# Head sums in two fp32r halves one pass later, and a read moved behind the inverse's copies, in a hybrid decoder layer

## The chip, the cores and the metric

The kernel runs on one core of a Trainium2 chip. The metric is the device time of one execution in microseconds (us). Engines are named as the profile names them: PE is TensorE, PEld its weight loads, DVE is VectorE, ACT is ScalarE, POOL is GpSimd, SP issues the DMAs.

## What is computed

One layer of a hybrid decoder, on 512 prompt tokens and 8 x 8 sample tokens (576 in all), width 1024, 8 heads. Cut to what matters here:

```
h = rmsnorm(x); proj = h @ w_in            # q|k|v | beta | decay | z | GLU input (2x) | gates a, b
q, k, v = silu(causal_conv4(proj)); q, k = l2norm(q) * 128**-0.5, l2norm(k)
per head, chunks of tokens:  lhs = I + strict(beta * k k^T * decay)
    u = solve(lhs, beta * v) - ...;  S = gl * S + ko^T u;  o = qd S + (q k^T * decay) u
o = o * rsqrt(mean(o*o) + eps) * delta_norm_g * silu(z)
c = causal_conv31(glu); o_b = silu(layernorm(c))
x = x + rmsnorm((sigmoid(a)*o + sigmoid(b)*o_b) @ w_out)
y = x + rmsnorm(relu(rmsnorm(x) @ w_up)**2 @ w_down)
```

## The kernel before

Channels lie on the 128 partitions, tokens along the free dimension, in two halves of 288 columns. Each projection is a **job**: 48 matmuls of 128x288, for each half 8 blocks of channels times three products (high weight by high input, low by high, high by low, all fp32r). Even halves of all jobs share one PSUM bank and odd halves another (`dense_ps`), so the first matmul of a job's half waits until the same half of the job before has been read (`act_read`), and half 0 also for its weights (`w_high` by ACT, `w_low` by POOL).

The head recurrence runs in **passes** `phase(n)`, n = 1 to 8, one for each head, beside the projection of the next head: passes 1 to 7 carry 7 jobs (q, k, v, then CA and CB, the two GLU halves, then Z and GA), pass 8 carries 10. A pass has 32 **slots** s, 2 us each or so. In slot s each engine runs what stands for it there, in program order: PE first issues `MIDDLE_AT[s]` dense matmuls, then the head's step. Passes 2 to 7 on PE, ACT, POOL and 4 to 7 on DVE are a loop. The steps that the text needs:

- Slot 0: PE sums k's squares over channels with a matrix of ones (`ones_pair`, two fp32r halves, L775 and L776), ACT makes the factor by Ln and Exp (L1490, L1492), DVE scales k (L1905). Slot 2: transposes of k and v on PE (L868 and on), DVE makes `gk`.
- Slots 8 to 21: the inverse of the 64x64 blocks, level by level. On even slots PE multiplies `t_r` by a level's part of the matrix (L920, at level 7 in slot 18 L918), ACT copies the product to `x_r`; on odd slots PE multiplies by `x_r` (L940, at slot 19 L938), DVE subtracts from `t_r` and transposes. In slot 18 ACT copies `x_r` (L1511) and then `u_r` (L1514), for which PE waits at L938.
- Slots 22 to 30: the chunks of the recurrence. The output o stands in PSUM; ACT copies it and squares it, DVE adds to the squares (slot 30, `o_sq`). In slot 30 PE makes the sample states' update (L1015), which DVE adds to `ss` (`sample_state`). In slot 31 PE sums o's squares with `ones_sum`, one fp32 product for each half (L768), ACT makes the factor (L1568, L1570) and q's squares (L1389), DVE scales o in two operations.
- ACT reads each job's halves in the slot after they are done: half 0 in `evac_first`, half 1 in `evac`. Half 0 of job 4 (CB, by a sigmoid) is read in slot 18, ahead of `x_r` and `u_r`. Its reader's table is loaded ahead of it.
- DVE works off the 31 taps of the Conformer convolution of the prompt (L1908, 128x512) in portions set by the tables `early` (the last taps of the head before) and `late` (the first taps of this one); passes 1, 2, 3 and 8 have tables of their own. The samples' taps are multiplied on POOL in two halves (slots 10 and 14; 2 and 4 in pass 8) and summed by a DVE reduction over 31 (L2036; slots 14 and 16, or 3 and 6).

In slot 19 of the loop PE has eleven dense matmuls. The last of them is the first of job 5, and behind it stands L938:

```order
L734 REGISTER_ALU
L743 ISA [waits w_low,w_high]
L749 MATMUL ps<-in_hi,w_hi 128x288 [waits act_read]
L931 REGISTER_ALU [waits x_ready]
L938 MATMUL ps<-x_r,u_r 64x64 [waits uc_ready]
L938 MATMUL ps<-x_r,u_r 64x64 x3
```

It is the row with `act_read`: for it half 0 of job 4 must have been read. The changed kernel has the same order here.

## Time and profile before

| | us |
|---|---|
| three runs | 1057.59, 1057.67, 1058.25 |
| median | 1057.67 |
| the profiled execution | 1057.45 |
| its span, first to last instruction | 1055.7 |
| PE busy in the span | 1038.3 |
| DVE, POOL, ACT busy | 745.4, 634.6, 592.1 |

So 1.75 us of the profiled execution lie outside the span. Passes 1 to 8 end at 116.7, 186.7, 252.5, 317.9, 383.3, 448.7, 514.0 and 598.1 us, if the start of L1015 is taken as the end; behind them come the output projection and the feed-forward part. The granted TensorE clock is 1.000 of full speed throughout. Matmuls overlap in the records, so distances between starts tell what one costs: dense matmuls start 0.13 us apart.

### The profile page before, as it was taken

The page shows a single profiled execution, that of the slowest core. Times are in us where ns is not written, and L with a number is a line of the kernel's source. Part 1 is how long each engine was busy: PE and PEld are TensorE (multiplying, and loading weights), DVE is VectorE, ACT ScalarE, POOL GpSimd, SP SyncE. Part 2 cuts the span into 40 slices and gives each one's busy share as a digit, 9 for nine tenths or more (in the row PEclk, how much of TensorE's full clock was granted, in tenths as well). Part 3 has the DMA queues.
Part 4 walks back from the last instruction along what each step waited for, and adds up shares of the span by engine and source line. Part 5 has one row for each costly group of instructions (what it writes and reads, how often), then busy time and mean ns, then how long its engine had stood idle before and what let it go on. Part 6 is the DMA issues. An engine that isn't in the chain of part 4 may idle for free.

```text
span 1055.7 us, 21847 instructions
## 1 busy us (share of the span) xinstructions
PE 1038.3 (98%) x7971; PEld 1012.8 (96%) x7971; DVE 745.4 (71%) x1254; ACT 592.1 (56%) x1105; POOL 634.6 (60%) x546
## 2 busy tenths in 40 slices
PE   8999999999999999999999999999999999999997
PEld 6999989999999999999999999999999999999997
DVE  7989898898888988889867757594544444444335
ACT  7855556575565755656646865765444443343632
POOL 1894686684876948768583443646555555555631
PEclk9999999999999999999999999999999999999999
DMA  6312212222122221322222162122222223222402
GB/s 239 105 68 81 95 42 92 84 80 95 40 91 84 79 95 40 93 81 90 88 77 61 43 250 80 41 70 97 98 96 81 81 83 114 82 79 79 116 7 89
DMA packets 32651, 92.08 MB, mean 87 GB/s; under 512 B 4688, under 2 KB 12240, under 8 KB 32592
## 3 DMA queue, kind: packets, MB, share of 16 engines
q1 hardware_dynamic: 32592, 91.29, 26.2%
q8 instruction: 37, 0.61, 0.2%
q14 instruction: 22, 0.18, 0.1%
HBM read 82.76 MB, written 8.52 MB: 86 GB/s over the span
## 4 chain that ended last, share of the span: by engine, by line
PE 80%; DVE 7%; POOL 4%; issue 3%; ACT 2%; DVEq 0%; ACTq 0%; POOLq 0%
PE ps L749 26%; PE ps L1162 15%; PE ps L1110 13%; PE ps L758 7%; PE ps L1194 5%; PE ps L714 3%; DVE ps L1908 3%; DVE t_r L1905 1%; PE ps L1006 1%; POOL in_lo L2601 1%; DVE work L2139 1%; PE ps L768 1%; POOL work L2601 1%; POOL w_lo L2601 1%; POOL o_a L2601 1%
## 5 line engine op out<-in xcount | busy, mean ns | idle before, releaser
L2601 POOL TENSOR_TENSOR w_lo<-raw,w_hi 128x1024 fp32r<-128x1024 f32 x100 | 241.2, 2414 | 157.0 <-ACT w_hi L1734 50.2
L749 PE MATMUL ps<-in_hi,w_hi 128*128 128x288 f32 x944 | 286.1, 303 | 1.1 <-ACT work L1408 0.6
L749 PE MATMUL ps<-in_lo,w_hi 128*128 128x288 f32 x944 | 282.3, 300 | 0.7 <-POOL in_lo L2601 0.7
L749 PE MATMUL ps<-in_hi,w_lo 128*128 128x288 f32 x944 | 282.7, 300 | 0.0
L1908 DVE SCALAR_TENSOR_TENSOR ps<-work,ct,ps 128x512 f32<-128x512 f32 x240 | 180.5, 752 | 7.1 <-DVE work L2068 1.6
L749 PEld LDWEIGHTS ps<-in_hi,w_hi 128*128 128x128 f32 x944 | 177.7, 188 | 2.7 <-issue 1.2
L749 PEld LDWEIGHTS ps<-in_lo,w_hi 128*128 128x128 f32 x944 | 177.3, 188 | 1.0 <-POOL in_lo L2601 0.9
L749 PEld LDWEIGHTS ps<-in_hi,w_lo 128*128 128x128 f32 x944 | 177.6, 188 | 0.5
L1905 DVE TENSOR_TENSOR o_a<-o_a,ps 128x576 f32<-128x576 f32 (+1 forms) x63 | 42.8, 681 | 107.3 <-PE ps L1162 73.1
L2601 POOL TENSOR_TENSOR w_lo<-t_pair,w_hi 128x1024 fp32r<-128x1024 f32 x18 | 43.6, 2422 | 42.5 <-ACT w_hi L1763 29.7
L1291 ACT CAST w_hi<-raw 128x1024 fp32r<-128x1024 f32 x63 | 65.6, 1043 | 0.2
L1162 PE MATMUL ps<-f_hi,w_lo 128*128 128x288 f32 x288 | 61.8, 296 | 0.0
L1162 PE MATMUL ps<-f_hi,w_hi 128*128 128x288 f32 x288 | 61.8, 296 | 0.0
L1162 PE MATMUL ps<-f_lo,w_hi 128*128 128x288 f32 x288 | 61.8, 295 | 0.0
L1908 DVE SCALAR_TENSOR_TENSOR ps<-work,qt,ps 128x512 f32<-128x512 f32 x72 | 54.0, 751 | 1.8
L2601 POOL TENSOR_TENSOR work<-work 128x576 f32<-128x576 f32 (+3 forms) x37 | 47.1, 1283 | 11.1 <-PE ps L996 7.9
L1162 PEld LDWEIGHTS ps<-f_hi,w_lo 128*128 128x128 f32 x288 | 46.3, 189 | 0.0
L1162 PEld LDWEIGHTS ps<-f_lo,w_hi 128*128 128x128 f32 x288 | 46.3, 189 | 0.0
L1162 PEld LDWEIGHTS ps<-f_hi,w_hi 128*128 128x128 f32 x288 | 46.2, 189 | 0.0
L1905 DVE TENSOR_TENSOR t_pair<-raw 128x1024 f32<-128x1024 f32 x24 | 45.1, 1880 | 0.0
L1734 ACT CAST w_hi<-raw 128x1024 fp32r<-128x1024 f32 x18 | 18.9, 1052 | 46.4 <-PE ps L1162 37.3
L1905 DVE TENSOR_TENSOR q_sq<-ps,q_sq 128x288 f32<-128x288 f32 x24 | 11.0, 458 | 47.4 <-PE ps L1110 46.9
(396 smaller groups left out, 2862.3 us busy)
## 6 DMA issues: line engine op xcount, KB each, us to landing
raw<-w_all_in SPq DMA_DIRECT2D x135, 512.0 KB, 3.7
work<-s_in_in SPq DMA_DIRECT2D x8, 512.0 KB, 3.4
s_sample_out<-work SPq DMA_DIRECT2D x8, 512.0 KB, 2.6
xt<-x_t_in SPq DMA_DIRECT2D x4, 576.0 KB, 6.4
xt<-x_t_in SPq DMA_DIRECT2D x2, 1152.0 KB, 7.1
y_out<-o_a SPq DMA_DIRECT2D x14, 144.0 KB, 1.9
halo<-halos_in SPq DMA_DIRECT2D x9, 156.0 KB, 3.5
conf_rows_out<-c_rows SPq DMA_DIRECT2D x8, 135.0 KB, 3.4
```

The costliest lines, as they stand in the source:

```text
L714: r = mm(ps[:, 2 * w + h, 0:HALF], a[:, k], b[:, k, h * HALF:(h + 1) * HALF], start=k == 0 and p3 == 0, stop=k == KB - 1 and p3 == 2)
L749: t = mm(dense_ps(n, j, h), a[:, w, k], b[:, k, h * HALF:(h + 1) * HALF], start=r == 0, stop=r == PASS_MM // 2 - 1)
L758: r = mm(dst, a[:, k], half_of(b[:, k], h), start=k == 0 and p3 == 0, stop=k == KB - 1 and p3 == 2)
L768: r = mm(dst[:, h], ones_r[:].bitcast(F32), src[:, h * HALF:(h + 1) * HALF], start=start, stop=stop)
L1110: r = mm(dst, a[:, k], b[:, k], start=start and k == 0 and p3 == 0, stop=k == 3 and p3 == 2, skip_group_check=True)
L1162: r = mm(job_ps(i % 2)[:, h], a[:, k], half_of(b[:, 4 * odd + k], h), start=k == 0 and p3 == 0, stop=k == 3 and p3 == 2)
L1194: r = mm(half_ps(i % 4), a[:, k], half_of(b[:, k], h), start=i < 2 * H - 1 and k == 0 and p3 == 0, stop=k == ks_end and p3 == 2, skip_grou ...
L1291: nc.scalar.copy(w_hi[:, w_buf(n, j)], raw[:, raw_slot(n, j)]).then_inc(w_high, 1)
L1734: nc.scalar.copy(ring(s)[0], raw[:, slot]).then_inc(w_high, 1)
L1905: return ve.tensor_tensor(out, a, b, op)
L1908: return ve.scalar_tensor_tensor(out=out, in0=a, scalar=s_, in1=b, op0=op0, op1=op1)
L2601: return gp.tensor_tensor(out, a, b, op)
```

## The change

The line numbers of the profile are of the kernel before.

```
+        osq_hi = ... [P, TOK] F32R at starts["vt"];  osq_lo = ... at starts["qn"]
@@ PE, slot 0 @@
+                            pe.wait_ge(o_sq, 2 * n - 2)
+                            pe.wait_ge(o_read, 5 * n - 5)
+                            ones_pair(g2(2), osq_hi, osq_lo).then_inc(o_sums, 1)
@@ PE, slot 2 @@
+                        if not n_is(n, 1):
+                            pe.wait_ge(o_log, n)
...
-                    if s == (30 if last(n) else 31):
+                    if last(n) and s == 30:
@@ ACT @@
-                for s in range(33):
+                def read_first(s):
                     pos, j = evac_first(n, s)
...
+                for s in range(33):
+                    if last(n) or s != 18:
+                        read_first(s)
...
+                    if s == 18 and not last(n):
+                        read_first(s)
...
-                    if s == (11 if last(n) else 24 if n_is(n, 1) else 19):
+                    if s == (11 if last(n) else 25 if n_is(n, 1) else 19):
...
                         A(g2(0), g2(0), ACT.Exp, scale=-0.5).then_inc(k_scale, 1)
+                        if not n_is(n, 1):
+                            act.wait_ge(o_sums, n - 1)
+                            A(two(v["at"]), g2(2), ACT.Ln, ...).then_inc(o_log, 1)
+                            act.wait_ge(o_log, n)
+                            A(v["at"], v["at"], ACT.Exp, scale=-0.5).then_inc(o_scale, 1)
+                            square_q(n - 1)
...
                     if s == 31 and not last(n):
+                        act.wait_ge(o_sq, 2 * n - 1)
+                        A(osq_hi[:], v["gk"][:, 0:TOK], ACT.Copy).then_inc(o_read, 1)
                         log_exp()
-                        act.wait_ge(o_sums, n)
-                        A(two(v["at"]), g2(2), ACT.Ln, ...).then_inc(o_log, 1)
-                        act.wait_ge(o_log, n + 1)
-                        A(v["at"], v["at"], ACT.Exp, scale=-0.5).then_inc(o_scale, 1)
-                        square_q(n)
@@ DVE @@
-                ve.tensor_reduce(..., conf_products(), ...)
+                ve.tensor_reduce(..., conf_products()[:, :, :, CF_TAPS // 2:CF_TAPS], ...)
+            def squares_low(n):
+                dve.wait_ge(o_read, 5 * n)
+                tt(osq_lo[:], v["gk"][:, 0:TOK], osq_hi[:].bitcast(F32), ALU.subtract).then_inc(o_sq, 1)
-                if s == 31 and not last(n):
...
+            def scale_head(n):
+                dve.wait_ge(o_scale, n)
...
+                tt(v["db"], o, v["at"], ALU.mult).then_inc(o_scaled, 1)
...
+                stt(o, v["db"], pcol("delta_g", 0), v["zs"], ALU.mult, ALU.mult).then_inc(head_out, 1)
...
                 if s == 30 and not last(n):
                     sample_state(n)
+                    squares_low(n)
...
+                    if not n_is(n, 1) and s == 1:
+                        scale_head(n - 1)
-            early = {1: 4, 2: 1, 3: 2, 8: 1, 14: 1, 16: 1}
+            early = {0: 1, 1: 1, 2: 2, 3: 2, 8: 2, 14: 1, 16: 2, 18: 1}
-            early_2 = {1: 4, 2: 2, 3: 2, 8: 2, 9: 1, 10: 1, 12: 1, 14: 1, 16: 1, 18: 2}
+            early_2 = {0: 1, 1: 1, 2: 2, 3: 2, 8: 2, 9: 1, 12: 1, 14: 2, 16: 2, 18: 4}
@@ POOL, behind the samples' products @@
+                        pool.wait_ge(conv31_p, 4 * n - 3 + 2 * half)
+                        m_ = CF_TAPS // 2
+                        tt(conf_products()[:, :, :, m_:2 * m_], conf_products()[:, :, :, m_:2 * m_],
+                           conf_products()[:, :, :, 0:m_], ALU.add).then_inc(conv31_p, 1)
```

The sum of o's squares moves from slot 31, as fp32, to slot 0 of the next pass, as two fp32r halves: ACT writes the high half in slot 31, DVE the low half behind `sample_state`. K's factor and scaling now come ahead of o's. The late tables lose a tap or two (`late` 21 to 19, `late_1` 14 to 13, `late_2` 19 to 17) and the early ones gain as many. The samples' products are added pairwise on POOL, 15 of 31, and DVE reduces 16. In pass 8, where o's squares stay fp32, DVE runs the head's step ahead of the layer norm's in each slot, and ACT squares behind the copies of the inverse.

On ACT, slot 18 of the loop, before and after. The conversion of job 6's weights leads, the read of job 4's half 0 is the sigmoid L1397, L1404 in the new numbering:

```order
L1291 CAST w_hi<-raw 128x1024 [waits job_done,raw_landed2]
L1438 REGISTER_ALU
L1397 ACT_TABLE_LOAD [waits zs_ready]
L1397 ACTIVATE work<-ps 128x288 [waits job_done]
L1511 ACTIVATE x_r<-ps 64x4x64 [waits x_ps]
L1514 ACTIVATE u_r<-work 64x4x64 [waits ui_ready]
L1514 ACTIVATE u_r<-work 64x4x64
```

```order
L1298 CAST w_hi<-raw 128x1024 [waits job_done,raw_landed2]
L1523 ACTIVATE x_r<-ps 64x4x64 [waits x_ps]
L1526 ACTIVATE u_r<-work 64x4x64 [waits ui_ready]
L1526 ACTIVATE u_r<-work 64x4x64
L1445 REGISTER_ALU
L1404 ACT_TABLE_LOAD [waits zs_ready]
L1404 ACTIVATE work<-ps 128x288 [waits job_done]
```

The table load and the read now stand behind the three copies to `x_r` and `u_r`.

On PE, at the end of the loop's body, before and after, with the dense matmuls of slot 0 left out behind the first:

```order
L1015 MATMUL ps<-work 128x512 [waits s_ready,um_ready]
L1015 MATMUL ps<-work 128x512
L768 MATMUL ps<-work,ones_r 128x288 [waits o_read,o_sq]
L768 MATMUL ps<-work,ones_r 128x288
L1041 REGISTER_ALU
L1041 COMPARE_AND_BRANCH
L749 MATMUL ps<-in_hi,w_hi 128x288 [waits act_read,w_low,w_high]
```

```order
L1022 MATMUL ps<-work 128x512 [waits s_ready,um_ready]
L1022 MATMUL ps<-work 128x512
L1048 REGISTER_ALU
L1048 COMPARE_AND_BRANCH
L751 MATMUL ps<-in_hi,w_hi 128x288 [waits act_read,w_low,w_high]
```

L768 is gone from between the state's update (L1015, now L1022) and the first dense matmul. In slot 0, behind the dense matmuls, there is now, from the last of k's four on:

```order
L778 MATMUL ps<-ksq_lo,ones_r 128x288
L777 MATMUL ps<-osq_hi,ones_r 128x288 [waits o_read,o_sq]
L778 MATMUL ps<-osq_lo,ones_r 128x288
L777 MATMUL ps<-osq_hi,ones_r 128x288
L778 MATMUL ps<-osq_lo,ones_r 128x288
```

The four matmuls on `osq` are new here; k's four stood here alone before, as L775 and L776.

On DVE, from `sample_state` in slot 30 on (128x1024), at the end of the loop's body, before and after:

```order
L1905 TENSOR_TENSOR work<-work,ps 128x1024 [waits ss_decayed,ss_ps]
L2028 REGISTER_ALU
L1908 SCALAR_TENSOR_TENSOR ps<-work,ct,ps 128x512 [waits conv31]
L2028 REGISTER_ALU
L1908 SCALAR_TENSOR_TENSOR ps<-work,ct,ps 128x512 [waits conv31]
L1905 ISA [waits o_scale]
L1905 TENSOR_TENSOR work<-o_a,work 128x576
L1908 SCALAR_TENSOR_TENSOR o_a<-work,par 128x576 [waits zs_ready,o_scaled]
```

```order
L1921 TENSOR_TENSOR work<-work,ps 128x1024 [waits ss_decayed,ss_ps]
L1921 TENSOR_TENSOR osq_lo<-work,osq_hi 128x576 [waits o_read]
L2044 REGISTER_ALU
L1924 SCALAR_TENSOR_TENSOR ps<-work,ct,ps 128x512 [waits conv31]
L2044 REGISTER_ALU
L1924 SCALAR_TENSOR_TENSOR ps<-work,ct,ps 128x512 [waits conv31]
L2337 REGISTER_ALU
L2337 COMPARE_AND_BRANCH
L1921 TENSOR_TENSOR work<-work,ps 128x576 [waits k_scale]
```

The new `osq_lo` comes directly behind `sample_state`. Before, o's two operations (`o_scale`, `o_scaled`) stood here; now the last row, k's scaling of the next pass, is ahead of them, and they stand behind two more taps.

## Rows read from the trace of the kernel before

**Rows 1.** The page, busy time, share of the span and instructions of PE.

```profile
PE 1038.3 (98%) x7971; PEld 1012.8 (96%) x7971; DVE 745.4 (71%) x1254; ACT 592.1 (56%) x1105; POOL 634.6 (60%) x546
```

**Rows 2.** Stretches, passes 1, 2, 5, 8: length, busy PE, PEld, DVE, ACT, POOL, clock.

```profile
48.00:116.67 68.67, 65.65 (x519) 62.98 (x517) 61.05 (x113) 42.88 (x89) 53.11 (x63) 1.00 0.24 80
116.67:186.66 69.99, 67.20 (x525) 63.51 (x524) 61.58 (x110) 38.78 (x82) 47.68 (x52) 1.00 0.22 75
...
317.90:383.30 65.40, 65.12 (x525) 63.44 (x524) 57.76 (x104) 38.79 (x82) 46.12 (x52) 1.00 0.25 78
...
514.04:598.06 84.02, 82.80 (x652) 80.93 (x651) 59.96 (x103) 57.63 (x101) 51.38 (x38) 1.00 0.24 77
```

**Rows 3.** Waits, all engines: who waited for whom, us in total, times, longest.

```profile
PE ps L938 <- ACT u_r L1514: 1.6, 6, 0.3
PE ps L980 <- DVE work L1908: 0.7, 1, 0.7
```

**Rows 4.** Timeline at the end of pass 5: start, us, engine, line, operation.

```profile
384.35 1.24 PE L768 MATMUL ps<-work,ones_r 128*128 128x288 f32 x4
384.47 1.22 DVE L1905 TENSOR_TENSOR work<-work,ps 128x1024 f32<-128x1024 f32 x1 [0.93 <-PE ps L1015]
385.21 0.51 PE L749 MATMUL ps<-in_hi,w_hi 128*128 128x288 f32 x1
385.56 0.30 PE L749 MATMUL ps<-in_hi,w_lo 128*128 128x288 f32 x1
387.01 0.30 PE L775 MATMUL ps<-ksq_hi,ones_r 128*128 128x288 f32 x1
...
387.54 0.29 PE L749 MATMUL ps<-in_hi,w_hi 128*128 128x288 f32 x1
```

**Rows 5.** Timeline, pass 6: DVE's step of slot 9, PE's of slot 10.

```profile
408.77 0.21 DVE L1905 TENSOR_TENSOR work<-work,ps 64x64 f32<-64x64 f32 x1
...
409.08 0.43 PE L920 MATMUL ps<-t_r,x_last 128*64 128x128 f32 x4
```

**Rows 6.** Timeline, pass 6, slots 18 and 19, of ACT and PE.

```profile
423.40 1.28 ACT L1397 ACT_TABLE_LOAD   x1
424.33 0.37 PE L918 MATMUL ps<-t_r,x_last 128*64 128x64 f32 x4
424.69 0.41 ACT L1397 ACTIVATE work<-ps 128x288 f32<-128x288 f32 x1
425.13 0.38 ACT L1511 ACTIVATE x_r<-ps 64x256 fp32r<-64x256 f32 x1
425.53 0.85 ACT L1514 ACTIVATE u_r<-work 64x256 fp32r<-64x256 f32 x2
...
425.95 0.29 PE L749 MATMUL ps<-in_hi,w_hi 128*128 128x288 f32 x1
426.52 0.39 PE L938 MATMUL ps<-x_r,u_r 128*64 128x64 f32 x4 [0.28 <-ACT u_r L1514]
```

**Rows 7.** Timeline, pass 8, the same step, where ACT has no read ahead of it.

```profile
564.33 0.39 PE L918 MATMUL ps<-t_r,x_last 128*64 128x64 f32 x4 [1.22 <-issue]
564.76 0.38 ACT L1511 ACTIVATE x_r<-ps 64x256 fp32r<-64x256 f32 x1 [1.24 <-PE ps L918]
...
566.03 0.41 ACT L1399 ACTIVATE gate<-ps 128x288 f32<-128x288 f32 x1
```

**Rows 8.** Timeline of PE, pass 2, slots 5 and 12.

```profile
132.83 0.40 PE L749 MATMUL ps<-in_hi,w_hi 128*128 128x288 f32 x1 [0.57 <-ACT work L1408]
...
149.07 0.43 PE L920 MATMUL ps<-t_r,x_last 128*64 128x128 f32 x4 [0.65 <-issue]
```

**Rows 9.** Groups by form: count, busy us, mean ns of one, idle before.

```profile
L1908 DVE SCALAR_TENSOR_TENSOR ps<-work,ct,ps 128x512 f32<-128x512 f32 x240 | 180.5, 752 | 7.1 <-DVE work L2068 1.6
L2036 DVE TENSOR_REDUCE work<-work 128x32 f32<-128x992 f32 x16 | 19.0, 1185 | 1.0 <-POOL work L2601 0.6
L2601 POOL TENSOR_TENSOR work<-work 128x576 f32<-128x576 f32 x16 | 22.7, 1417 | 3.1 <-ACT work L1397 3.1
```

More of the change, by code:

```diff
@@ L189, in build @@
         ksq = v["extk"][:, 4:4 + TOK]
+        osq_hi = nc.alloc_sbuf_tensor_at("osq_hi", [P, TOK], F32R, offset=work_at + 4 * (5 * SEQ + starts["vt"]))
+        osq_lo = nc.alloc_sbuf_tensor_at("osq_lo", [P, TOK], F32R, offset=work_at + 4 * (5 * SEQ + starts["qn"]))
         q_sq = sb("q_sq", TOK)
@@ L1475, in phase @@
                         A(job_ps(1), job_ps(1), ACT.Copy, scale=1.0 / D).then_inc(mu_ready, 1)
-                    if last(n) and 15 <= s < 19:
-                        for k in (2 * s - 30, 2 * s - 29):
-                            act.wait_ge(xc_ready, k + 1)
-                            A(xc_squares(k), conf[:, k], ACT.Square).then_inc(xc_sq, 1)
                     if last(n) and s == 21:
@@ L1492, in phase @@
                         A(g2(0), g2(0), ACT.Exp, scale=-0.5).then_inc(k_scale, 1)
+                        if not n_is(n, 1):
+                            act.wait_ge(o_sums, n - 1)
+                            A(two(v["at"]), g2(2), ACT.Ln, scale=1.0 / P, bias=con("epsq")).then_inc(o_log, 1)
+                            act.wait_ge(o_log, n)
+                            A(v["at"], v["at"], ACT.Exp, scale=-0.5).then_inc(o_scale, 1)
+                            square_q(n - 1)
                     if s == 2 and not n_is(n, 1):
@@ L1524, in phase @@
                             conv_silu(n, 0)
+                    if s == 18 and not last(n):
+                        read_first(s)
+                    if last(n) and 15 <= s < 19:
+                        for k in (2 * s - 30, 2 * s - 29):
+                            act.wait_ge(xc_ready, k + 1)
+                            A(xc_squares(k), conf[:, k], ACT.Square).then_inc(xc_sq, 1)
                     if s == 22:
@@ L1562, in phase @@
                         A(dst, g(3), ACT.Copy).then_inc(o_read, 1)
-                        act.wait_ge(o_read, 4 * n - 1)
+                        act.wait_ge(o_read, 5 * n - 2)
                         A(g(3), g(3), ACT.Square).then_inc(o_read, 1)
                     if s == 31 and not last(n):
+                        act.wait_ge(o_sq, 2 * n - 1)
+                        A(osq_hi[:], v["gk"][:, 0:TOK], ACT.Copy).then_inc(o_read, 1)
                         log_exp()
-                        act.wait_ge(o_sums, n)
-                        A(two(v["at"]), g2(2), ACT.Ln, scale=1.0 / P, bias=con("epsq")).then_inc(o_log, 1)
-                        act.wait_ge(o_log, n + 1)
-                        A(v["at"], v["at"], ACT.Exp, scale=-0.5).then_inc(o_scale, 1)
-                        square_q(n)
             act.preload_act_table_set("sigmoid_and_others")
@@ L2034, in conf_samples @@
                 at = SEQ + half * n_ * LS
-                dve.wait_ge(conv31_p, 2 * h + half + 1)
-                ve.tensor_reduce(v["c31"][:, at:at + n_ * LS].rearrange("p (s a) -> p s a", s=n_), conf_products(),
+                dve.wait_ge(conv31_p, 4 * h + 2 * half + 2)
+                ve.tensor_reduce(v["c31"][:, at:at + n_ * LS].rearrange("p (s a) -> p s a", s=n_),
+                                 conf_products()[:, :, :, CF_TAPS // 2:CF_TAPS],
                                  mybir.AxisListType.X, ALU.add).then_inc(conv31_s, 1)
@@ L2237, in phase @@
                 for s in range(32):
+                    if last(n) and 22 <= s < 26:
+                        for k in (2 * s - 44, 2 * s - 43):
+                            if k == 0:
+                                dve.wait_ge(ln_scale, 2)
+                            tt(two(conf[:, k]), two(conf[:, k]), job_ps(1), ALU.mult).then_inc(ln_scaled, 1)
+                    if n_is(n, 1) and s == 0:
+                        dve.wait_ge(in_ready, KB)
+                    head(n, s)
                     if last(n) and 14 <= s < 18:
@@ L2246, in phase @@
                         tt(xc_squares(k), xc_squares(k), xc_squares(k + 1), ALU.add).then_inc(xc_pair, 1)
-                    if last(n) and 22 <= s < 26:
-                        for k in (2 * s - 44, 2 * s - 43):
-                            if k == 0:
-                                dve.wait_ge(ln_scale, 2)
-                            tt(two(conf[:, k]), two(conf[:, k]), job_ps(1), ALU.mult).then_inc(ln_scaled, 1)
-                    if n_is(n, 1) and s == 0:
-                        dve.wait_ge(in_ready, KB)
-                    head(n, s)
                     if not n_is(n, 1) and s == 0:
```

31 lines of the change are left out of this document (14 added, 17 removed).

## The prediction

> **What bounds the kernel now.** The page comes first: PE is busy in 1038.3 of the 1055.7 us of its span [rows 1]. So an edit counts only by what it does to PE's own work and to the places where PE stands still. The stretches by pass say where those are. A steady pass (5) takes 65.4 us with 0.28 us of PE idle; pass 1 has 3.0 us idle, pass 2 takes 4.6 us more than pass 5 and has 2.8 us idle, and pass 8 has 1.2 us [rows 2]. These are idle times of the pipelined records, and the distances between starts show somewhat more. The waits name the steady one: L938 waits for ACT's u_r, 0.3 us six times [rows 3]. In the timeline L938 starts 0.57 us behind the dense matmul ahead of it, where a head step otherwise follows at the dense step of 0.13 us, so the true stop is 0.44 us [rows 6]. The other engines have room.
>
> **o's sum (7 passes).** L768 starts at 384.35 and the second dense matmul behind it at 385.56, 1.21 us. Without it a dense step of 0.13 and the change from fp32 to fp32r, for which I take 0.15, are left, so it costs 0.93. The four fp32r matmuls that replace it cost what k's four cost, 387.54 - 387.01 = 0.53 [rows 4]. Gain 0.40 a pass, **-2.8 us**; bounds 0.3 to 0.55. Does PE wait for them? sample_state ends at 385.69; osq_lo behind it, priced as a tap of 0.75 [rows 9], ends at 386.45. PE would come to o's sum at 387.01 - 0.93 + 0.53 = 386.6 [rows 4]. It just fits; 0.2 us later it would not. ACT's new copy and the factor of o stand behind k's factor, where PE's next use of the bank is slot 2, some 3 us on: nothing.
>
> **What DVE gives back of it.** In slot 9 DVE's last step on the samples ends at 408.98 and PE's L920 starts at 409.08: PE runs at DVE's pace there [rows 5]. DVE comes to it with nearly as much work as before: osq_lo and a second tap in slot 8 are new, three taps ahead of slot 2 are gone and one is added in slot 2. I take DVE 0.2 us earlier and PE 0.4, so 0.2 is lost in each of the five steady passes: **+1.0 us**; bounds 0 and the whole 2.8.
>
> **The read behind the copies (7 passes).** This is the large term. Before, ACT loads the sigmoid's table at 423.40, while it waits anyway, and reads job 4's half 0 from 424.69 to 425.10, then copies x_r and u_r until 426.38 [rows 6]. Now the copies come first. When would they? Pass 8 shows this step without a read ahead: L1511 starts 0.43 us behind L918's start, and the next read on ACT 1.70 us behind it, with no table to load [rows 7]. So in passes 1 to 7 the load starts at L918 + 1.70, lasts until + 2.98, and the read of 0.41 ends at + 3.40. The copies alone would be ready for L938 by + 1.66, where PE is at + 1.75: the old stop of 0.44 would go. But the last dense matmul of slot 19, ahead of L938, is job 5's first and waits for this read. PE reaches it at 425.95 - 424.33 = 1.62 behind L918; with the 0.14 us from ACT's end to PE's start (426.38 to 426.52) it can start only at + 3.54 [rows 6]. PE stands 1.92 us, and L938 follows at + 3.67 instead of + 2.19. Net 1.48 us a pass, seven times: **+10.4 us**. Nothing hides it, since PE is the bound and its queue is in order. In pass 2 four taps of 0.75 in slot 18, two more than before, keep DVE busy to about the same point, so PE's next head steps come no earlier there either. Bounds: 1.2 if ACT's steps run tighter together, 1.6 if PE restarts more slowly.
>
> Of the table the trace shows that the activation behind it starts 1.29 us after it began (423.40 to 424.69), the load's own 1.28 and no more [rows 6]. The Trainium skill ("ScalarE: Activation LUTs", What ACT_TABLE_LOAD costs) has about 1283 ns for the load and a drain of about 1380 ns with every switch. By the page the stop would be 1.38 us longer each time, and the sum 9.7 us higher.
>
> **Pass 1.** L980 waits 0.7 us for DVE [rows 3]; the new stop of 1.9 us ahead of it gives DVE the time to catch up, and a tap leaves slot 10. I take **-1.0 us** of the 3.0 idle [rows 2]; bounds 0 and -2.
>
> **Pass 2, ahead of slot 18.** It loses its time because DVE is late. At 132.83 a dense matmul starts 0.57 us late since ACT, held by DVE's difference, reads its bank late; at 149.07 L920 comes 0.65 late, behind a tap too many in slot 10 [rows 8]. The change brings k's scaling forward by some 2 us (o's factor and scaling are no longer ahead of it), takes the tap out of slot 10, and halves the reductions of 1.19 us [rows 9]. Of the 4.6 us over pass 5 [rows 2] about 0.9 lie behind slot 18; of the other 3.7 I take **-3.0 us**; bounds -1.5 and -3.7.
>
> **Pass 8.** L918 waits 1.22 us [rows 7] for DVE's t_r, which stood behind two layer-norm subtractions and a sum of pairs. They now come behind it, but the variance chain behind is as long, and L953 stands at its end: **-0.8 us**; bounds 0 and -1.4.
>
> **POOL's additions.** 480 elements a partition, between a third and all of the 1.42 us of 576 [rows 9], twice a pass. Behind the second stands the low half of job 5's weights, which DVE's shorter reduction lets start earlier. Nothing on PE: 0, bounds 0 and +2.
>
> Sum: -2.8 + 1.0 + 10.4 - 1.0 - 3.0 - 0.8 = **+3.8 us**. The profiled execution took 1057.45 us, its span 1055.7 and 1.75 around it; with the sum 1061.25. It is 0.2 below the median of 1057.67, which would give 1061.5. I say 1061.3.
>
> **Rivals.** *The read is in time.* If ACT's read were over before PE needs the bank, 1.62 us behind L918, the stop would not come and the old one of 0.44 would go in six passes, -2.6, while pass 2's taps keep +1.4. Then -2.8 + 1.0 - 1.2 - 1.0 - 3.0 - 0.8 = -7.8, **1049.7**, faster. For it: the change is made at just the place where PE waits for u_r. Against: the order of ACT and of PE around it, and 1.70 + 1.28 + 0.41 against 1.62. It decides at a read that ends 1.5 us behind L918. Chance 0.12.
>
> *The stops heal each other.* The 1.9 us stop in passes 1 and 2 lets DVE catch up wholly, the sum's gain is kept, pass 8 gains all: -2.8 + 10.4 - 2.2 - 4.6 - 1.4 = -0.6, **1056.9**, within 0.2%. For it: all three passes wait for DVE. Against: the stop is late in the pass, and what is lost ahead of it is lost. Chance 0.10.
>
> *DVE and POOL are later still.* The sum's gain is given back whole at slot 10 (+1.8), pass 2 gains half: 3.8 + 1.8 + 1.5 = +7.1, or with POOL's bound +9: **1066**. Chance 0.10.
>
> *A drain with the table.* A switch of tables also waits for the pipeline to empty, behind copies that have only just ended: 3.8 + 7 x 1.38 = +13.5, **1071**. Against: the 1.29 us of the row, though there ACT had nothing fresh in its pipe. Chance 0.03. It is the page's rule on the drain, and by that rule the trace does not agree.
>
> **How the numbers follow.** Forecast 0.65, centre 1061.3, from its bounds 1058 to 1065. The range 1056.5 to 1066.5 holds the forecast, the healed case and most of the slow one. It leaves out the read in time, the drain and half of the slow case, about 0.2. A measurement of this kernel tells some 0.2% (2.1 us) from no change. Faster: 0.12 and a little of the healed case, 0.14. Same: the rest of that and the forecast's lower edge, 0.13. Slower 0.73.
>
> **What would show it.** In the changed profile: the dense matmul ahead of the step on x_r and u_r in slot 19 waits for ACT's sigmoid read, 1.6 to 2 us by start distances, seven times; a steady pass takes 65.4 - 0.2 + 1.5 = 66.7 us, pass 2 about 68.3, pass 1 about 69; the four matmuls on osq follow k's at 0.13 us each with no gap; pass 8's wait at level 7 is gone. It is wrong if steady passes come out below 65.4: then ACT's read was not what PE waited for.

## The result, and the profile after

The changed kernel took **1084.57 us** in the median of its runs (1084.21 to 1086.61), beside 1057.84 (1057.59 to 1058.25) for the kernel before on the same chip: ratio 1.0256, 95% interval 1.0238 to 1.0274. The prediction said slower, but 1061.3 us, and its range ended at 1066.5.

The profiled execution of the changed kernel took 1084.21 us, its span is 1082.4, 26.7 more than before. Of its page the row of PE, which answers [rows 1]:

```profile
PE 1045.0 (97%) x7971; PEld 1019.0 (94%) x7971; DVE 754.5 (70%) x1261; ACT 594.9 (55%) x1112; POOL 659.2 (61%) x562
```

PE's busy time grew by 6.7 us although it has the same number of matmuls and cheaper ones, and 20 us are new idle time. Busy time that grows with the same work points to a slower clock. The stretches by pass, which answer [rows 2] (length, busy PE, PEld, DVE, ACT, POOL, then the granted clock), show where:

```profile
48.00:121.48 73.48, 67.15 (x522) 64.94 (x520) 60.87 (x114) 43.18 (x89) 57.17 (x65) 0.98 0.23 75
121.48:191.46 69.98, 66.62 (x524) 63.36 (x523) 61.42 (x110) 39.29 (x83) 49.41 (x54) 1.00 0.23 75
191.46:259.12 67.66, 65.54 (x525) 63.38 (x524) 59.80 (x107) 39.20 (x83) 49.38 (x54) 1.00 0.23 76
259.12:326.09 66.97, 65.16 (x524) 63.33 (x523) 58.36 (x105) 39.20 (x83) 49.40 (x54) 1.00 0.23 77
326.09:394.71 68.62, 66.78 (x524) 64.92 (x523) 58.47 (x105) 39.19 (x83) 49.38 (x54) 0.98 0.23 75
...
463.31:530.38 67.07, 65.25 (x524) 63.38 (x524) 58.40 (x105) 39.20 (x83) 49.38 (x54) 1.00 0.24 76
530.38:624.39 94.01, 85.15 (x652) 83.00 (x651) 66.24 (x105) 57.85 (x102) 54.10 (x40) 0.95 0.22 69
```

Passes 1 to 8 are 4.8, 0.0, 1.8, 1.6, 3.2, 3.2, 1.7 and 10.0 us longer than before, and what is behind them 0.4. Two kinds of steady pass stand side by side, 67 us and 68.6, and the second kind has a clock below 1.00. Pass 8 alone has more than a third of the loss.

**The steady stop.** Pass 5, slots 18 and 19, of ACT and PE, the rows that answer [rows 6]:

```profile
368.13 0.84 ACT L1526 ACTIVATE u_r<-work 64x256 fp32r<-64x256 f32 x2
368.99 1.28 ACT L1404 ACT_TABLE_LOAD   x1
370.29 0.41 ACT L1404 ACTIVATE work<-ps 128x288 f32<-128x288 f32 x1
368.82 0.29 PE L751 MATMUL ps<-in_lo,w_hi 128*128 128x288 f32 x1
370.75 0.40 PE L751 MATMUL ps<-in_hi,w_hi 128*128 128x288 f32 x1 [1.64 <-ACT work L1404]
370.99 0.37 PE L945 MATMUL ps<-x_r,u_r 128*64 128x64 f32 x4
```

The dense matmul behind 368.82 starts 1.93 us later instead of 0.13, since the read of job 4 now stands behind the copies and the table load: 1.80 us of stop, and its predecessor's records end 1.64 before it. It comes in each of passes 1 to 7. The activation starts 1.30 us behind the start of its table load, and the load 0.02 us behind the end of fresh copies: the load's own 1.28 and no more. The Trainium skill ("ScalarE: Activation LUTs", What ACT_TABLE_LOAD costs) has a drain of about 1380 ns with every switch; this trace does not agree, and the rival built on it did not come.

**What follows the stop.** The granted clock of PE, in stretches of 5 us behind the stop of pass 5 (the clock is the third figure from the end), and dense matmuls there:

```profile
370.00:375.00 5.00, 4.25 (x26) 4.25 (x27) 2.88 (x5) 4.36 (x8) 4.29 (x5) 0.68 0.60 211
375.00:380.00 5.00, 5.00 (x41) 5.00 (x41) 4.21 (x7) 1.62 (x6) 4.25 (x4) 0.98 0.29 97
```

```profile
372.02 0.44 PE L751 MATMUL ps<-in_hi,w_lo 128*128 128x288 f32 x1
372.26 0.44 PE L751 MATMUL ps<-in_lo,w_hi 128*128 128x288 f32 x1
```

The matmuls start 0.24 us apart instead of 0.13: PE runs at 1.2 GHz, the lower of its two levels, for some 3 us. By distances between starts against the kernel before this costs 1.6 us. It came behind the stops of passes 1, 5 and 6, not behind those of 2, 3, 4 and 7, and PE also came out of the long stop of pass 8, below, at the lower level.

**Pass 8.** Slots 0 to 2. First the three engines that stand behind the stop, then PE:

```profile
536.73 2.54 POOL L2626 TENSOR_TENSOR work<-masks,hc 128x512 f32<-128x512 bf16 x4 [4.33 <-DVE hc L2257]
539.23 2.33 POOL L2626 TENSOR_TENSOR w_lo<-raw,w_hi 128x1024 fp32r<-128x1024 f32 x1
541.53 2.10 POOL L2626 TENSOR_TENSOR work<-work,ct 128x992 f32<-128x992 f32 x1
543.71 1.46 POOL L2626 TENSOR_TENSOR work<-work 128x480 f32<-128x480 f32 x1
538.01 6.24 DVE L1921 TENSOR_TENSOR work<-o_a,work 128x576 f32<-128x576 f32 x1
544.28 1.50 DVE L1924 SCALAR_TENSOR_TENSOR o_a<-work,par 128x576 f32<-128x576 f32 x1
545.86 1.28 ACT L1402 ACT_TABLE_LOAD   x1 [7.22 <-DVE o_a L1924]
547.71 0.58 PE L751 MATMUL ps<-in_hi,w_hi 128*128 128x288 f32 x1 [7.49 <-ACT work L1402]
```

In pass 8 the first job is Z. ACT may read it only when head 7 has been scaled, since the scaling multiplies by the old silu(Z). Before, DVE scaled in slot 31 of pass 7; now it does so in slot 1 of pass 8. That alone would cost something. But DVE's first product, of o by its factor, lasted **6.24 us** where it lasts 0.76 before, and the operation behind it 1.50 instead of 0.82. POOL is at work all the while, from 536.73 on without a pause until 543.63. In passes 2 to 7, where only the four products of the masks run beside it, the same product lasts 1.62:

```profile
331.94 3.06 POOL L2626 TENSOR_TENSOR work<-masks,hc 128x512 f32<-128x512 bf16 x4 [3.83 <-DVE hc L2257]
333.22 1.63 DVE L1921 TENSOR_TENSOR work<-o_a,work 128x576 f32<-128x576 f32 x1
```

So my theory was: (a) seven stops at the read; (b) a half clock behind some stops; (c) DVE's product, which has two inputs in SBUF, is held while POOL works, 0.87 us a pass and 5.5 in pass 8; (d) something in pass 1. The rivals: the clock falls have a cause of their own, and the product is slow for another reason than POOL.

### The profile page after: what moved, and what is told of

The parts are those of the page before. It is cut to its first block, busy times and chain, and to the rows that moved or that the text cites. A ratio compares the mean times of both kernels' runs of the same rounds, so it can differ in the third digit from the quotient of the medians.

```text
span 1082.4 us, 21930 instructions
## 1 busy us (share of the span) xinstructions
PE 1045.0 (97%) x7971; PEld 1019.0 (94%) x7971; DVE 754.5 (70%) x1261; ACT 594.9 (55%) x1112; POOL 659.2 (61%) x562
## 4 chain that ended last, share of the span: by engine, by line
PE 82%; DVE 6%; POOL 3%; ACT 3%; issue 2%; DMA 1%; ACTq 0%; POOLq 0%; DVEq 0%
PE ps L751 29%; PE ps L1169 14%; PE ps L1117 12%; PE ps L760 5%; PE ps L1201 5%; PE ps L716 3%; DVE ps L1924 2%; DVE work L1921 2%; PE ps L1013 1%; POOL in_lo L2626 1%; POOL work L2626 1%; PE ps L927 1%; PE ps L947 1%; POOL o_a L2626 1%; PE ps L922 1%
## 5 line engine op out<-in xcount | busy, mean ns | idle before, releaser
L751 PE MATMUL ps<-in_hi,w_hi 128*128 128x288 f32 x944 | 289.0, 306 | 20.2 <-ACT work L1404 11.6
L2626 POOL TENSOR_TENSOR work<-work 128x576 f32<-128x576 f32 (+4 forms) x53 | 64.8, 1229 | 12.8 <-PE ps L1003 7.9
L1921 DVE TENSOR_TENSOR t_r<-t_r,ps 64x256 fp32r<-64x256 f32 x80 | 33.0, 413 | 15.6 <-PE ps L947 8.4
```

The source lines that it names most:

```text
L751: t = mm(dense_ps(n, j, h), a[:, w, k], b[:, k, h * HALF:(h + 1) * HALF], start=r == 0, stop=r == PASS_MM // 2 - 1)
L1921: return ve.tensor_tensor(out, a, b, op)
L2626: return gp.tensor_tensor(out, a, b, op)
```

## The experiments

All ratios are against the kernel before, run on the same chip, with 95% intervals.

**The read ahead of the copies again.** One part of the change undone:

```diff
-                    if last(n) or s != 18:
-                        read_first(s)
+                    read_first(s)
...
-                    if s == 18 and not last(n):
-                        read_first(s)
```

> The changed kernel with one part undone: ACT reads job 4's half 0 ahead of the copies of x_r and u_r again. Theory: the stop of 1.64 us at the dense matmul in slot 19 goes in all seven passes and the old wait of 0.44 us at the step on u_r comes back, 1.40 net by the offsets of the changed trace, 9.8 us in all; and the half clock of some 3.4 us behind the stop in passes 1, 5 and 6 (1.2, 1.55 and 1.55 us) is a consequence of the stop and goes too: 1084.6 - 9.8 - 4.3 = 1070.5. Rival: the clock falls have another cause and stay: 1074.8. Second rival: what is saved there is lost at the next wait for DVE in passes 1 and 2: 1073.

Measured 1075.49 us, 1.0168 (1.0151 to 1.0185): 9.1 less than the changed kernel, not 14. The stops at the read are gone and with them every fall of the clock in passes 3 to 7. Pass 7 as a stretch (length, PE busy, clock):

```profile
456.62:522.70 66.08, 65.43 (x524) 1.00 0.24 78
```

It gave 1.0 a pass and not 1.4, since the stop had let DVE catch up: without it, PE waits 0.2 us for DVE's `x_last`. In pass 2 this is large. The four taps of slot 18 now hold DVE's `t_r`, and the clock falls behind that wait (of this run, DVE, then PE):

```profile
163.34 3.13 DVE L1921 SCALAR_TENSOR_TENSOR ps<-work,ct,ps 128x512 f32<-128x512 f32 x4
168.77 1.63 PE L922 MATMUL ps<-t_r,work 128*128 128x128 f32 x7 [2.27 <-DVE t_r L2158]
```

So the falls follow stops of PE, and the second rival of this run was right in part.

**The table ahead, the read behind.** Only the load moves:

```diff
+                    if s == 18 and not last(n):
+                        act.preload_act_table_set("sigmoid_and_others")
```

> The changed kernel with the sigmoid's table loaded in slot 18 ahead of the copies of x_r and u_r, the read still behind them. Theory: the stop shrinks by the load's 1.28 us to about 0.36 in all seven passes, -9.0, and a stop of that length is followed by no half clock, -4.3: 1071.3. Rival: the clock falls have nothing to do with the stop's length: 1075.6. Second rival: the load delays the copies, and PE waits for u_r as well: 1078.

Measured 1074.30 us, 1.0154 (1.0137 to 1.0171). The stop shrank to 0.35 us in passes 4 and 5, no clock fell in passes 3 to 7, and a steady pass took 66.1. Of the stop, 1.28 us were the table. That it is not 1071 has the reasons of the run above: a steady pass gained 0.9 us beside the clock and not 1.3, pass 2 got a wait of 1.88 us for DVE's `t_r` with a half clock behind it and grew by 1.1, and in pass 1 the clock fell behind the wait of 2.08 us at L987 instead.

**The factor in PSUM.** DVE's product reads one of its inputs from PSUM:

```diff
-                            A(v["at"], v["at"], ACT.Exp, scale=-0.5).then_inc(o_scale, 1)
+                            A(g2(2), two(v["at"]), ACT.Exp, scale=-0.5).then_inc(o_scale, 1)
...
-                            pe.wait_ge(o_log, n)
+                            pe.wait_ge(o_scaled, n - 1)
...
-                tt(v["db"], o, v["at"], ALU.mult).then_inc(o_scaled, 1)
+                tt(two(v["db"]), two(o), g2(2), ALU.mult).then_inc(o_scaled, 1)
```

> The changed kernel, with o's factor left in PSUM (the Exp writes the bank that the sum stood in) and DVE's first product of the scaling reading it there, so that one of its two inputs is not in SBUF. Theory: that product lasted 6.24 us in pass 8 (1.6 in passes 2 to 7) instead of 0.76 because POOL was at work on SBUF at the time; with the factor in PSUM it lasts 0.76 to 0.8 everywhere. In pass 8 the scaling ends at about 539.7 instead of 545.8, the table load and the read follow, and PE's stop shrinks from 7.5 to some 1.4 us: -6.1, and the half clock behind it goes, -2.3. In passes 2 to 7 DVE gains 0.87 us, and of the 0.68 that PE loses up to slot 10 some 0.5 come back, -3: 1073.2. Rival: the product is slow for another reason (its wait, o's columns): unchanged, 1084.6. Second rival: only pass 8 gains, since DVE's other work sets slot 10: 1076.2.

Measured 1080.90 us, 1.0221 (1.0204 to 1.0238), not 1073.2. The product lasts 0.75 in every pass. In pass 8 the *next* operation, by the gain and silu(Z), both in SBUF, was held in its place:

```profile
536.83 0.75 DVE L1921 TENSOR_TENSOR work<-o_a,ps 128x576 f32<-128x576 f32 x1
537.61 5.47 DVE L1924 SCALAR_TENSOR_TENSOR o_a<-work,par 128x576 f32<-128x576 f32 x1
```

So it is not that operation but any with two inputs in SBUF at that time, and pass 8 kept a stop of 5.97 us. The steady pass gained 0.7: pass 7 took 66.34 with its stop, against 67.07.

```profile
462.86:529.20 66.34, 64.69 (x524) 1.00 0.23 77
```

By distances between starts, PE stays 0.42 us ahead of the kernel before from the sums up to the stop, where in the changed kernel it had lost that and 0.2 more by slot 10. In time the profiled execution gained 3.0 us, less than 0.7 x 6, since in it the clock fell in five passes behind the same stops of 1.65 and not in three.

**POOL idle while DVE scales.** In pass 8 DVE copies the head's columns, which start POOL, behind the scaling. Both inputs stay in SBUF:

```diff
-                    if not n_is(n, 1) and s == 0:
+                    if not (n_is(n, 1) or last(n)) and s == 0:
                         head_cols(n)
...
+                    if last(n) and s == 1:
+                        head_cols(n)
```

> The changed kernel with one step of pass 8 moved: DVE copies the head's columns, for which POOL's work of slots 0 to 2 waits, behind the scaling of head 7 and not ahead of it. Both inputs of the product stay in SBUF. Theory: POOL is idle while the product runs, so it lasts 0.76 us instead of 6.24, and the stop of 7.5 us at PE's third half falls to about 1.4; the half clock behind goes: -8.4. POOL is some 1.6 us later with its masks and weights, which PE may feel by up to 1 us: 1076.2 to 1077.2. Rival: the product is held by something other than POOL: 1084.6 or worse by POOL's delay.

Measured 1079.17 us, 1.0194 (1.0177 to 1.0211). Of pass 8, DVE and POOL, and PE's stop:

```profile
540.53 0.75 DVE L1921 TENSOR_TENSOR work<-o_a,work 128x576 f32<-128x576 f32 x1
541.32 0.82 DVE L1924 SCALAR_TENSOR_TENSOR o_a<-work,par 128x576 f32<-128x576 f32 x1
542.31 2.53 POOL L2628 TENSOR_TENSOR work<-masks,hc 128x512 f32<-128x512 bf16 x4 [7.31 <-DVE hc L2257]
544.06 0.37 PE L751 MATMUL ps<-in_hi,w_hi 128*128 128x288 f32 x1 [1.24 <-ACT work L1402]
```

The same product on the same operands lasts 0.75 with POOL idle and 6.24 with POOL busy. Together the two runs show the cause. The Trainium skill ("SBUF — State Buffer", SBUF: two separate sides) says that VectorE and GpSimd share one pair of ports, which a GpSimd operation that reads SBUF, or a VectorE operation with two SBUF inputs, holds for the whole instruction while the other is blocked; the traces agree. What they add is that in pass 8 DVE was not let in between POOL's operations: it waited through four that followed each other (two mask products, the weights' low half, the samples' products) and came in where POOL waited for its own result. That is no rule. In passes 2 to 7 of the changed kernel DVE was let in between two mask products that followed each other: the last of them, 64x64, then took 0.81 us instead of 0.28, and DVE lost only 0.87. What decides between the two stays open.

I could have known of the hold from the kernel before. In its pass 8, POOL's product on `t_r` lasted 2.66 us from 567.39 on, beside DVE's sums of pairs, where it lasts 1.09 to 1.12 in passes 1 to 7, and the third of these sums 1.53 instead of 0.74. Both engines are held, in turn.

Pass 8 took 87.28 us instead of 94.01. It lacks 1.6 us of what was expected because POOL, started later, held PE's first step of the inverse for 1.62 us. Neither behind the stop of 1.24 us nor behind that of 1.62 did the clock fall.

**The read behind the copies, alone.** The kernel before, with only that part of the change:

```diff
-                for s in range(33):
-                    pos, j = evac_first(n, s)
+                def read_first(s):
+                    pos, j = evac_first(n, s)
...
+                for s in range(33):
+                    if last(n) or s != 18:
+                        read_first(s)
...
+                    if s == 18 and not last(n):
+                        read_first(s)
```

> The kernel before with one part of the change alone: in slot 18 of passes 1 to 7 ACT reads job 4's half 0 behind the copies of x_r and u_r. Theory: the stop of 1.65 us comes at the last dense matmul of slot 19 in seven passes, 1.4 net each, 9.9 us; behind a stop of this length the clock fell in three of seven passes in the changed kernel, in four or five in its variants, at 1.6 us each, so 5 to 8 us more: 1072.5 to 1076, middle 1074. Rival: the half clock needs the changed kernel's other stops: 1067.7.

Measured 1074.21 us, 1.0151 (1.0135 to 1.0166). Pass 3 and pass 6:

```profile
190.95:258.30 67.35, 65.44 (x525) 1.00 0.23 76
...
395.12:463.52 68.40, 66.75 (x525) 0.98 0.23 75
```

Pass 3 is 1.47 us longer than before: the stop alone, as it was predicted (1.48). Pass 6 is 3.0 longer: the stop and a half clock. That fell behind the stops of passes 1, 4, 5, 6 and 7. This part alone, one read moved, costs 16.4 us, more than half of the change's loss; seven stops at 1.47 are 10.3 of them, and the other 6 are the clock.

**A longer stop.** A second table load ahead of the sigmoid's:

```diff
                     if s == 18 and not last(n):
+                        log_exp()
                         read_first(s)
```

> The changed kernel with a second table load (that of Ln and Exp) ahead of the sigmoid's in slot 18 of passes 1 to 7, which makes the stop of 1.65 us one of 2.93. Theory: a longer stop is always followed by half clock, so it comes in all seven passes and not in three, at 1.6 us each: 1084.6 + 7 x 1.28 + 4 x 1.6 = 1100. Rival: the half clock does not depend on the stop's length: 1093.6.

Measured 1095.88 us, 1.0367 (1.0350 to 1.0384). PE's stretches of 5 us at or just behind the stops of passes 3, 4, 5, 6 and 7 (busy, clock):

```profile
240.00:245.00 5.00, 4.58 (x29) 0.70 0.59 210
310.00:315.00 5.00, 4.67 (x24) 0.53 0.61 210
380.00:385.00 5.00, 3.24 (x18) 0.69 0.70 223
450.00:455.00 5.00, 3.38 (x31) 1.00 0.68 245
520.00:525.00 5.00, 5.00 (x44) 1.00 0.65 210
```

The stops are 2.94 us long, and the clock fell in passes 1, 3, 4 and 5, not in 2, 6 and 7. My theory that a longer stop is always followed by half clock is wrong. Over all runs it followed 22 of the 35 stops of 1.64 to 1.75 us, 4 of these 7, 5 of 6 waits of 2.08 us in pass 1, the two waits of 1.88 and 2.27 us in pass 2, one of 1.57 in pass 8, all six stops of 5.97 to 7.5 us, none of the three waits of 1.62 us for POOL in pass 8, none of the three of 1.5 us in pass 2 of later runs, and none of 1.24 us or less. Between 1.5 and 3 us nothing that I changed decides it; what does stays open.

**Pass 1.** The Conformer read of head 0 back in slot 24:

```diff
-                    if s == (11 if last(n) else 25 if n_is(n, 1) else 19):
+                    if s == (11 if last(n) else 24 if n_is(n, 1) else 19):
```

> The changed kernel with one step of pass 1 back where it was: ACT reads the Conformer's sums of head 0 in slot 24 and not in slot 25. Theory: in slot 25 that read stands behind the k squares, for which ACT waits 2.28 us for POOL; so the next head's taps reach DVE late, five of them stand ahead of the chunk's step, and PE waits 2.08 us at L987. In slot 24 this wait shrinks to the 0.7 of before, and the 0.78 at L1001 goes: -2: 1082.5. Rival: it is the third tap of slot 22 that makes DVE late, and the read in slot 24 then holds the chunk's copy instead: 1084.5.

Measured 1083.83 us, 1.0241 (1.0226 to 1.0257). In the changed kernel the taps' weights of the next head come late because ACT's read stands behind the squares that wait for POOL (ACT, DVE, PE):

```profile
110.84 0.68 ACT L1387 ACTIVATE ksq_hi<-work 128x576 fp32r<-128x576 f32 x1 [2.28 <-POOL work L2626]
111.43 0.67 ACT L1477 ACTIVATE conf<-ps,ct 128x512 f32<-128x512 f32 x1
112.64 0.75 DVE L2042 TENSOR_SCALAR ps<-work,ct 128x512 f32<-128x512 f32 x1 [2.32 <-ACT ct L1483]
113.42 3.92 DVE L1924 SCALAR_TENSOR_TENSOR ps<-work,ct,ps 128x512 f32<-128x512 f32 x5
117.65 0.49 PE L987 MATMUL ps<-work 128*128 128x128 f32 x2 [2.08 <-DVE work L1924]
```

With the read in slot 24 the wait is 0.72 again, and pass 1 ends at 119.62 instead of 121.48, 1.9 us less, as expected. In time only 0.7 came, since in this execution the clock fell behind five of the seven stops at the read.

**Mending all of it.** Three versions take the read ahead of the copies, the factor in PSUM, the Conformer read in slot 24, and taps moved out of the way; the first two also start POOL behind the scaling in pass 8.

> The changed kernel with the four places mended that the theory names: the read ahead of the copies; o's factor in PSUM; in pass 8 the head's columns copied behind the scaling; in pass 1 the tables of taps and the slot of the Conformer read of before, and in pass 2 two taps fewer in slot 18 (two instead of four; one more in slot 10, one more at the end of pass 1). Theory, from the run with the read ahead (1075.5): passes 3 to 7 each 0.7 shorter, -3.5; pass 8 -6.5; pass 2's wait of 2.27 us at level 7 and the half clock behind it gone, -3.5; pass 1 -3.7: 1058.3, and pass lengths of 65.4 in the steady ones, with the offset of the sum's gain, 0.42, kept up to slot 18. Rival: the places shift into each other and half of it comes: 1067.

> As the run before it (four places mended), and in passes 4 to 7 the new tap of slot 18 goes back to slot 24 of the pass before, in pass 8 one of slot 9's. Theory: the tap of 0.75 us stands ahead of DVE's work for the step on x_last (0.2 us wait in the run with the read ahead, 0.4 in offsets): -0.4 us in four passes, so 1056.5, below before by 1.3. Rival: the tap in slot 24 costs as much: 1058.3.

> The kernel with the four places mended and the taps of slot 18 moved (1061.3), with more: in pass 8 the first product of the scaling goes to PSUM too, so that neither step has two inputs in SBUF, DVE copies the head's columns in slot 0 again, and ACT loads the silu's table ahead of its wait; in pass 1 the changed kernel's taps ahead of slot 21 with the read in slot 24; in passes 2 and 3 one tap each out of the way of the wait found there. Theory: pass 8 loses its stop of 1.23 us for the read and the 1.62 for POOL, -3.0; pass 2 the 0.8 for the scaling and 0.65 for the low half of the squares, -1.4; pass 3 -1.0; pass 1 -0.5: 1055.4, 0.9977 of before. Rival: POOL's work holds DVE's next step with two inputs in SBUF in pass 8, and the stop stays: 1058.

The new tables of the first, and behind the dots those that the second changes besides (`early_8` loses one tap of slot 9):

```diff
+            early_1 = {1: 3, 2: 2, 3: 2, 8: 1, 10: 1, 12: 1, 14: 1, 16: 1, 21: 5, 22: 2, 23: 2}
+            late_1 = {25: 3, 26: 3, 27: 2, 28: 1, 29: 1, 30: 3, 31: 1}
+            early_2 = {0: 1, 1: 1, 2: 2, 3: 2, 8: 2, 9: 1, 10: 1, 12: 1, 14: 2, 16: 2, 18: 2}
...
+            early = {0: 1, 1: 1, 2: 2, 3: 2, 8: 2, 14: 1, 16: 2}
+            late = {21: 3, 22: 2, 23: 2, 24: 4, 25: 2, 26: 2, 27: 1, 28: 1, 29: 1, 30: 1, 31: 1}
```

Measured 1062.43 (1.0043, 1.0030 to 1.0057), 1061.31 (1.0032, 1.0020 to 1.0044) and 1058.41 (1.0007, 0.9998 to 1.0016). The first has steady passes of 65.4, the second of 65.2, which is 0.2 less than before: the tap in slot 18 did cost that. Both have 87.27 in pass 8, where the late POOL holds PE. The third writes DVE's first product to PSUM in pass 8 as well,

```diff
+                            pe.wait_ge(head_out if last(n) else o_scaled, n if last(n) else n - 1)
...
+                            if last(n):
+                                act.preload_act_table_set("silu_and_others")
                             act.wait_ge(head_out, n)
...
+                mid = g2(2) if n_is(n, H - 1) else two(v["db"])
+                tt(mid, two(o), g2(2), ALU.mult).then_inc(o_scaled, 1)
...
+                stt(two(o), mid, pcol("delta_g", 0), two(v["zs"]), ALU.mult, ALU.mult).then_inc(head_out, 1)
```

starts POOL early again and loads the silu's table ahead of the wait, and moves single taps in passes 1 to 3; neither operation was held (0.76 and 0.82), and pass 8 fell to 84.54. All three stayed above what was expected (1058.3, 1056.5, 1055.4), mostly in pass 2: it took 70.09, 70.11 and 70.83 us, where some 67.5 was expected of the first and a further 1.4 less of the third.

**Pass 2, and the last sum of pass 8.** Against the third of them:

```diff
+            late_1 = {25: 3, 26: 3, 27: 2, 28: 1, 29: 2, 30: 1, 31: 1}
+            early_2 = {0: 1, 1: 1, 2: 2, 3: 2, 8: 2, 9: 1, 10: 1, 12: 1, 14: 2, 16: 2, 18: 3}
...
-                    if last(n) and s == 19:
-                        for i, (a, b) in enumerate(((0, 2), (4, 6), (0, 4))):
+                    if last(n) and s in (19, 20):
+                        for i, (a, b) in ((0, (0, 2)), (1, (4, 6))) if s == 19 else ((2, (0, 4)),):
```

> The kernel mended further (1058.4), with the changed kernel's taps at the end of pass 1 (13) and 18 in pass 2, of which three stand in slot 18 and one in slot 10; and in pass 8 the last of the four sums of pairs behind DVE's step on x_last instead of ahead of it. Theory: in pass 2 the low half of o's squares is no longer behind two more taps, so PE's 0.65 us at its sum goes, and the lead of 2 us that the changed kernel has before slot 18 comes back in part, 1.5 us of it given up at level 7: pass 2 takes 69.6 instead of 70.83. Pass 8's wait of 1.03 at x_last becomes 0.4: in all 1056.6. Rival: DVE's work as a whole sets pass 2, and the taps only move the wait: 1058.

Measured 1060.20 (1.0025, 1.0016 to 1.0034). Pass 2 came as expected, 69.84. But pass 8 grew to 87.4. Its last sum of pairs, two inputs in SBUF, now ran beside POOL (DVE, then PE with the sum's matmuls at half clock):

```profile
570.69 2.22 DVE L1920 TENSOR_TENSOR work<-work 128x576 f32<-128x576 f32 x1
573.06 2.26 PE L770 MATMUL ps<-work,ones_r 128*128 128x288 f32 x4 [1.57 <-DVE work L1920]
```

I had moved one operation past a point without asking what POOL does there: the same mistake again, and a third time that the hold shows.

**Without POOL's additions.** The third of the mended versions, with the reduction of before:

```diff
-                        pool.wait_ge(conv31_p, 4 * n - 3 + 2 * half)
-                        m_ = CF_TAPS // 2
-                        tt(conf_products()[:, :, :, m_:2 * m_], conf_products()[:, :, :, m_:2 * m_],
-                           conf_products()[:, :, :, 0:m_], ALU.add).then_inc(conv31_p, 1)
...
-                                 conf_products()[:, :, :, CF_TAPS // 2:CF_TAPS],
+                                 conf_products(),
```

> The kernel mended further (1058.4) without POOL's two additions a pass: DVE's reduction runs over all 31 products again. Theory: nothing on PE in the steady passes, which stay at 65.2; where DVE is late (passes 1 and 2) 0.3 to 0.5 us more each: 1058.4 to 1059.4. Rival: the additions cost something, since POOL's next product or DVE's steps with two inputs in SBUF wait for them: 1057 or less.

Measured 1058.44 (1.0005, 0.9996 to 1.0014), as expected the same. Steady passes took 65.09 instead of 65.21, pass 2 71.59 instead of 70.83. So the additions cost 0.1 us a steady pass and give 0.8 where DVE is late.

**The parts together, and the changed order with its neighbours moved.** The first has the third mended version's pass 8 and the two tables of the diff above for passes 1 and 2.

> The kernel mended further (1058.4) with the taps of the run named e12 in passes 1 and 2 (13 at the end of pass 1, 18 in pass 2), and pass 8 as in the kernel mended further. Theory: the two passes add up as they were measured apart, 69.84 for pass 2 and 84.5 for pass 8: 1057.4. Rival: the gain of pass 2 is lost behind it: 1058.4.

> The kernel before it (read ahead of the copies) with the changed kernel's order of the read behind the copies of x_r and u_r, but the sigmoid's table loaded ahead of them, and job 5's first matmul, which waits for the read, moved from the end of slot 19 to slot 20, behind the step on x_r and u_r. Theory: what was wrong with the new order is only what stands around it. The copies are ready 0.4 us earlier, PE takes the step on them at once, and the read ends while the step runs: neither the old wait of 0.44 nor the stop of 1.65 is left, -0.4 us in six passes: 1055.0. Rival: the read still ends later than PE needs it, 0.3 us a pass, or DVE, which stands behind the same step, gives nothing back: 1057.4 or more.

The second differs from the first in ACT's slot 18, as the diff with the table ahead shows, and in one number for PE:

```diff
-MIDDLE_AT = (12, 12, 14, 14, 14, 14, 12, 13, 12, 10, 10, 12, 10, 13, 11, 13, 12, 11, 11, 11, 8, 8,
+MIDDLE_AT = (12, 12, 14, 14, 14, 14, 12, 13, 12, 10, 10, 12, 10, 13, 11, 13, 12, 11, 11, 10, 9, 8,
```

Measured 1057.23 (0.9993, 0.9984 to 1.0002), as expected, and 1057.89 (1.0000, 0.9991 to 1.0009) instead of 1055.0: the rival came. In the second PE waits neither for the read nor for `u_r` (ACT and PE):

```profile
425.01 0.41 ACT L1404 ACTIVATE work<-ps 128x288 f32<-128x288 f32 x1
425.13 0.39 PE L945 MATMUL ps<-x_r,u_r 128*64 128x64 f32 x4
425.59 0.38 PE L751 MATMUL ps<-in_hi,w_hi 128*128 128x288 f32 x1
```

What is gained there is waited for later; the waits of the two runs (first the one with the read ahead, then the other) say for whom:

```profile
PE ps L960 <- DVE x_last L1920: 1.5, 3, 1.0
...
PE ps L945 <- ACT u_r L1527: 1.2, 5, 0.2
```

```profile
PE ps L960 <- DVE x_last L1925: 3.2, 8, 1.0
```

A steady pass takes 65.2 in both. So the order of read and copies itself costs nothing; what cost was the table behind the copies and the waiting matmul ahead of the step. Nor does it gain anything, because DVE is the next in line. No version beat the kernel before by more than its measurement tells: what is saved, 0.2 us in each steady pass, passes 1 and 8 take, in the first of the two 0.5 us each; by what in them is not shown.

## Why the prediction was wrong

- **o's sum: right.** Forecast -0.40 a pass. Pass 4 of the changed kernel is 0.42 ahead at its first dense matmul behind the sums, 3.82 us behind the pass's start against 4.24 before (262.94 and 259.12, before 387.54 [rows 4] and 383.30). The osq matmuls followed k's at 0.13 us with no gap, so `osq_lo` did fit. The 0.15 us in the sum for the change from fp32 to fp32r stood in no row; with it the sum came within 0.02.
- **What DVE gives back: wrong in size.** Forecast 0.2 us in each of five passes, with all of the sum's gain as the bound; measured 0.64 by slot 10 (0.5 of it by slot 8), beyond the bound, so +3.2 instead of +1.0. The step that failed is "DVE comes to it with nearly as much work as before": I counted DVE's instructions, at durations from places where POOL is idle. Moved into slot 1, the product runs beside POOL's masks and takes 1.62. The run with the factor in PSUM showed it: with 0.75 there, nothing is lost up to slot 18.
- **The read behind the copies: right as far as it went.** Forecast 1.92 us of stop and 1.48 net; measured 1.80 and 1.41 (L945 44.85 us behind the pass's start against 43.22 before, less the 0.22 late at slot 10), seven times, +9.9 against +10.4. Counted from the step of level 7, as in the forecast, L945 follows at + 3.68 in passes 4 to 7, where + 3.67 was forecast. In the kernel before it cost 1.47.
- **The clock: not in the sum at all.** The row of before said 1.000 throughout, and I took it as given. Three falls behind these stops cost 4.7 us, a fourth in pass 8 2.3. The term is as large as most that I did work out.
- **Pass 8: the largest error.** "ACT's new copy and the factor of o stand behind k's factor, where PE's next use of the bank is slot 2, some 3 us on: nothing" looks only at PE's use of the bank. The scaling of the head moves with the factor, past a pass's border, and in pass 8 ACT's read of Z waits for it. Instead of -0.8 pass 8 had +10.0: 7.75 of stop by distances (5.5 of it the held product, 0.7 the held operation behind it), 2.3 of clock, -0.45 for the sum, and for the layer norm -0.9 at level 7 [rows 7] but +1.2 at L960, where the last sums of pairs now hold `x_last`; I had named that chain and allowed 0.4 us for it.
- **Pass 1: wrong in sign.** Forecast -1.0 beside the stop; beside the stop (1.5) and the half clock (1.5) it was +1.8. The move of the Conformer read from slot 24 to 25, a one-figure edit, I had not followed along ACT's queue, past the squares.
- **Pass 2: half of it.** Forecast -3.0 ahead of slot 18 beside the sum; measured -1.5 beside it (1.93 ahead in all at L925). The stop then cost its 1.6, and four taps 0.35 more.
- **POOL's additions: right**, 0 within 0.1 a steady pass.

Together: -2.9 + 3.2 + 10.2 (the stops of passes 1 and 2 were a little longer) + 7.0 of clock + 1.8 - 1.2 + 8.0 (pass 8 without its clock, its sum's gain counted before) + 0.4 = 26.5 of the 26.7 us.

## What to carry over

When an operation moves, three things move with it: the instructions of other engines that wait for its result (also where a last pass has another order), what runs beside it, and the place where PE stands if it is late. A duration belongs to a place: before you use it elsewhere, look whether it has two inputs in SBUF and what POOL does at the new place. And a stop of PE of 1.64 us and more is not priced by its length alone: add the half clock that may follow it, here 1.6 us in six cases of ten at 1.64 to 1.75 us.
